# State-space layer of a hybrid encoder: the order of the setup's end, of the last group's gating and weight splits, and the place of the gate's store

## The chip, the cores and the metric
One Trainium2 chip, one core. The metric is device time in microseconds (us) of one execution of the whole two-layer network. Runs of one kernel shown below lie within 0.2% of each other.

## The reference, cut to what matters
Layer 0 is attention, layer 1 the bidirectional state-space mixer (Mamba-2 form), both with modulation before and a layer norm after:

```python
mod = cond @ ada_w[i] + ada_b[i]
shift, scale, gate = jnp.split(mod, 3, axis=-1)
h = x * (1.0 + scale[:, None, :]) + shift[:, None, :]
y = mixer(h)
x = _layer_norm(DEEPNORM_ALPHA * x + gate[:, None, :] * y, ln_g[i], ln_b[i])
```

```python
proj = h @ w_in                       # (1024, 2048 z + 3072 xBC + 64 dt)
xbc = silu(conv5(xbc) + conv_b)       # centred depthwise conv
dt_f, dt_b = softplus(...)            # one decay per head and direction
y = ssd(x, dt_f, B, C) + flip(ssd(flip(x), flip(dt_b), ...)) + d_skip * x
y = _rms_norm(y * jax.nn.silu(z), norm_w)
return y @ w_out                      # (2048 -> 1024)
```
The scan runs in 8 chunks of 128 tokens: inside a chunk `cb * lmat` (a masked product of C and B times a decay matrix) and across chunks a state that is decayed and added. There are 4 groups of 8 heads with a head size of 64 and a state of 128. All is float32.

## The kernel before
A float32 product is done as three matmuls of rounded parts: each operand is split in a rounded part (`w_hi`, `h_hi`, by ScalarE) and a remainder (`w_lo`, `h_lo`, by GpSimd or VectorE). Each engine has its own program, in the order in which the code issues it, with counting semaphores between them; all DMAs are issued by SP in one order.

**End of the attention layer.** For each of 8 tiles of 128 tokens VectorE, ScalarE and GpSimd normalise the projected tile; SP loads the residual rows (`load_x`, L393, buffer qT of two), stores the finished tile (L422), and behind tile 3 stores the next layer's gate (L427 to L430): 1024 values that lie on 128 partitions x 8 go to one row of 1024 in HBM, with `allow_slow_non_contiguous`. Only the very end of the kernel reads that row (L1783).

**Setup of the state-space layer.** TensorE projects 12 units (6 tiles of weights by 2 halves of the tokens) for group 0. ScalarE writes the centre tap (`first_centre`), VectorE adds the other taps (`first_unit`). Then, `for i in range(8)`, TensorE transposes one chunk (`unstage`), ScalarE copies it (`unstaged`), GpSimd scales it (`decayed_inputs`), TensorE makes the chunk's state (`state`) and VectorE adds it to the decayed one before (`update`, L2472). `update(0, k)` for k from 2 overwrites a buffer of hb that SP must have stored first (`keep_hb`, L1650). SP issues the weights w6 and w7 (`load_w`; w7 waits until w6 is split by GpSimd), and behind them the five stores of hb. `products` makes the products of C and B for four chunks each, `mask_products` (VectorE) masks them, `shift`, `lesser` and `exponentials` make the decay matrices, GpSimd's `weights_back` and VectorE's `weights` multiply the two. `skip` (ScalarE) puts d_skip * x into y.

**Groups.** A loop over groups 0 to 2 and the last one written out. Each goes through 8 chunks c; TensorE interleaves quarters of the next projections with each chunk's products (`quarter`, `outputs`). SP loads for chunk c+2 the decay rows (1 MB, L1637), the exponentials (L1643) and the stored hb (L1739). In the last group the quarters are those of z (8 units, `silu_half` on ScalarE and `silu_z` on VectorE).

**Behind the last group.** y is gated (8 instructions of VectorE, L2687), stored transposed (`send`), and loaded again tile by tile (`load_y(n)`, n counting pairs (m, c) of token tile and half of the channels in ORDER: (0,0), (1,0), (2,0), (0,1), (1,1), (2,1), (3,0), (3,1), ...). `split_y`/`y_rest` split it, `split_o`/`o_rest` split the 16 row blocks of w_out, `square` and GpSimd's `sum_squares` make the norm. TensorE's `out_products(m, k)` is 6 matmuls of 128 x 512. It first runs tiles 0, 1 and 2 together over k (blocks 0 to 15), as weights arrive, and then m = 3 to 7 one by one. A tile's accumulator `acc(m)` has two banks, of three pairs in turn; `normalise(m)` (L2724) reads it and frees it.

## Time and profile before

| | us |
|---|---|
| runs shown | 2201.43, 2200.47, 2197.43 (median 2200.47) |
| profiled execution, its time | 2194.47 |
| its span | 2192.7 |
| TensorE busy | 2094.6 (96%) |
| VectorE busy | 1035.6 (47%) |
| ScalarE busy | 948.0 (43%) |
| GpSimd busy | 832.9 (38%) |
| mean granted clock of TensorE | 0.993 |

Times inside the span are counted from its start. Engines in the rows: PE = TensorE, DVE = VectorE, ACT = ScalarE, POOL = GpSimd, SPq = SP's DMA queue. L12 is line 12 of the kernel before. "Busy" of TensorE comes from modelled ends of pipelined matmuls. The attention layer ends at about 1307 in the span, the setup at 1413, the groups follow at 1413.7, 1574 and 1735, the last one is at 1896 to 1985, and the output projection runs to the end.

### The profile page before, as it was taken

To read this page: it belongs to the slowest core of one execution; us is meant where nothing else is said; L and a number is where in the kernel's file an instruction comes from. 1 tells how busy PE (TensorE), PEld (TensorE's weight loads), DVE (VectorE), ACT (ScalarE), POOL (GpSimd) and SP (SyncE) were. 2 spreads that over 40 slices of the span, in tenths; PEclk is the share of its full clock that TensorE was granted. 3 is DMA by queue.
4 is the path that set the end of the run, shared out by engine and by line. 5 is a ranking of instruction groups with operands and counts; after the bars stand their busy time and mean duration, and the time that the engine had idled before them with its cause. 6 is when DMAs were issued, how large, how long until landed. Compare 5 with 4: busy or idle time off the path is not lost.

```text
span 2192.7 us, 33044 instructions
## 1 busy us (share of the span) xinstructions
PE 2094.6 (96%) x11587; PEld 1681.3 (77%) x11587; DVE 1035.6 (47%) x2305; ACT 948.0 (43%) x2354; POOL 832.9 (38%) x444
## 2 busy tenths in 40 slices
PE   4999999999999999999998989899999999998997
PEld 3888888887878888888776767688778778777776
DVE  6323223332233232232323566688487587477553
ACT  3243433434333343343435235565475565575220
POOL 0211141411412314114134163466376465484463
PEclk9999999999999999999999999999999999999998
DMA  7312221221222112112122341455254255356331
GB/s 306 129 39 66 58 71 38 69 67 30 67 67 69 67 39 59 67 51 85 38 62 66 119 116 53 139 166 163 94 181 154 104 164 157 105 182 214 141 113 58
DMA packets 98949, 221.26 MB, mean 101 GB/s; under 512 B 18850, under 2 KB 45090, under 8 KB 97316
## 3 DMA queue, kind: packets, MB, share of 16 engines
q1 hardware_dynamic: 98852, 219.98, 31.8%
q8 instruction: 59, 0.97, 0.2%
q14 instruction: 38, 0.31, 0.0%
HBM read 195.75 MB, written 24.19 MB: 100 GB/s over the span
## 4 chain that ended last, share of the span: by engine, by line
PE 68%; POOL 9%; issue 9%; DVE 7%; DMA 4%; ACT 3%; SPq 0%; POOLq 0%; DVEq 0%; ACTq 0%
PE pp L504 40%; PE pp_s L1926 7%; PE tp L536 4%; PE sp_ L526 3%; PE yo_p L2120 2%; PE op L609 2%; POOL rw L1824 2%; POOL trunk L1834 2%; POOL xw L1817 2%; PE pp_s L2120 1%; PE op L598 1%; DVE stage_s L2528 1%; POOL xd L1810 1%; PE tp L545 1%; DMA a_slot<-in_ada_w 1%
## 5 line engine op out<-in xcount | busy, mean ns | idle before, releaser
L437 POOL TENSOR_TENSOR w_lo<-w_raw,w_hi 128x1024 fp32r<-128x1024 f32 x80 | 190.6, 2382 | 847.6 <-ACT w_hi L765 847.6
L504 PE MATMUL pp<-h_hi,w_hi 128*128 128x512 f32 x1264 | 501.1, 396 | 0.1
L504 PE MATMUL pp<-h_hi,w_lo 128*128 128x512 f32 x1264 | 492.8, 390 | 0.0
L504 PE MATMUL pp<-h_lo,w_hi 128*128 128x512 f32 x1264 | 492.2, 389 | 0.0
L1035 DVE COPY probT<-tp 128x512 f32<-128x512 f32 x160 | 103.1, 685 | 544.9 <-PE tp L536 544.9
L1926 PE MATMUL pp_s<-h_hi,w_hi_s 128*128 128x512 f32 x624 | 270.7, 434 | 9.4 <-DVE stage_s L2528 7.4
L504 PEld LDWEIGHTS pp<-h_hi,w_hi 128*128 128x128 f32 x1264 | 237.4, 188 | 51.2 <-issue 4.8
L504 PEld LDWEIGHTS pp<-h_hi,w_lo 128*128 128x128 f32 x1264 | 237.2, 188 | 50.7
L504 PEld LDWEIGHTS pp<-h_lo,w_hi 128*128 128x128 f32 x1264 | 237.7, 188 | 46.7
L826 ACT ACTIVATE prob<-prob,mz 128x256 f32<-128x256 f32 (+2 forms) x384 | 169.9, 444 | 191.6 <-DVE mz L1015 191.6
L1926 PE MATMUL pp_s<-h_hi,w_lo_s 128*128 128x512 f32 x624 | 245.4, 393 | 0.0
L1926 PE MATMUL pp_s<-h_lo,w_hi_s 128*128 128x512 f32 x624 | 245.0, 393 | 0.0
L1926 PEld LDWEIGHTS pp_s<-h_hi,w_hi_s 128*128 128x128 f32 x624 | 117.9, 189 | 52.4 <-issue 26.7
L1575 POOL TENSOR_TENSOR w_lo_s<-w_raw_s,w_hi_s 128x1024 fp32r<-128x1024 f32 x40 | 104.8, 2619 | 122.8 <-ACT w_hi_s L1585 122.2
L2528 DVE SCALAR_TENSOR_TENSOR stage_s<-pp_s,gconv,stage_s 128x512 f32<-128x512 f32 (+2 forms) x184 | 137.8, 749 | 11.8 <-ACT stage_s L2168 6.1
L1926 PEld LDWEIGHTS pp_s<-h_lo,w_hi_s 128*128 128x128 f32 x624 | 118.1, 189 | 32.0 <-issue 10.6
L1926 PEld LDWEIGHTS pp_s<-h_hi,w_lo_s 128*128 128x128 f32 x624 | 117.8, 189 | 26.3
L1015 DVE CUSTOM_DVE_ANT_0 prob<-sp_,bias,slope 128x256 f32<-128x256 f32 (+2 forms) x384 | 134.3, 407 | 5.9 <-PE sp_ L526 3.6
L1035 DVE COPY v<-tp 128x512 f32<-128x512 f32 x48 | 30.9, 685 | 197.7 <-PE tp L545 197.7
L1817 POOL TENSOR_TENSOR xw<-trunk,fac 128x512 f32<-128x512 f32 x53 | 72.6, 1371 | 100.5 <-PE st_p L1941 88.7
L770 ACT ACTIVATE vT<-pp 128x512 f32<-128x512 f32 (+2 forms) x56 | 44.6, 812 | 137.2 <-PE pp L504 134.8
L2230 ACT ACTIVATE rw<-rw,fac 128x128 f32<-128x128 f32 x256 | 78.3, 389 | 41.4 <-DVE rw L2463 41.4
(453 smaller groups left out, 3547.7 us busy)
## 6 DMA issues: line engine op xcount, KB each, us to landing
w_raw<-in_a_w SPq DMA_DIRECT2D x80, 512.0 KB, 3.4
rw<-cum_rows SPq DMA_DIRECT2D x32, 1024.0 KB, 5.6
w_raw_s<-in_b_w SPq DMA_DIRECT2D x40, 512.0 KB, 3.5
ew<-exp_rows SPq DMA_DIRECT2D x64, 256.0 KB, 4.8
num_wide<-in_ada_w SPq DMA_DIRECT2D x16, 768.0 KB, 6.6
num_wide<-merge_rows SPq DMA_DIRECT2D x16, 768.0 KB, 7.8
yT_b<-trunk SPq DMA_DIRECT2D x32, 256.0 KB, 2.3
stage_s<-yT_b SPq DMA_DIRECT2D x16, 512.0 KB, 5.5
```

The costliest lines, as they stand in the source:

```text
L437: nc.gpsimd.tensor_tensor(w_lo[:, slot].rearrange("p k c -> p (k c)"), w_raw[:, slot].rearrange("p k c -> p (k c)"), w_hi[:, slot].rearran ...
L504: last = nc.tensor.matmul(pp[:, par, :], w[:, slot, k, :], keep[h][:, k, half * HALF:(half + 1) * HALF], start=(k == 0 and n == 0), stop=( ...
L536: last = nc.tensor.transpose(tp[:, par, c * P:(c + 1) * P], prob[:, u % 2, c * P:(c + 1) * P], ident[:])
L826: last = nc.scalar.activation(prob[:, u % 2, c:c + w], prob[:, u % 2, c:c + w], ACT.Exp, scale=-1.0, bias=mz[:, m:m + 1], accum_out=mz[:, ...
L1015: last = nc.vector.tensor_tensor_reduce(out=prob[:, u % 2, c:c + w], in0=sp_[:, u % 2, c:c + w], in1=bias[:, c0:c0 + w], scale=slope[:, h: ...
L1035: nc.vector.tensor_copy(dst, src).then_inc(t_free, 2 if ev[0] == "e" or ev[0] == "s" and last_pair else 1)
L1575: nc.gpsimd.tensor_tensor(flat(w_lo[:, slot]), flat(w_raw[:]), flat(w_hi[:, slot]).bitcast(F32), ALU.subtract).then_inc(S["lo_done"], 1)
L1817: nc.gpsimd.tensor_tensor(per_head(xw_of(n, k)), per_head(x[:, c, :]), bcast(f_in[:, c, d, :], HD), ALU.mult).then_inc(S["xw_ready"], 1)
L1926: last = nc.tensor.matmul(out, w[:, slot, k, :], of_h(h, k, half), start=(k == 0 and n == 0), stop=(k == KT - 1 and n == 2))
L2120: ins = nc.tensor.matmul(acc(m, half), y, w[:, half * HALF:(half + 1) * HALF], start=(k == 0 and i == 0), stop=(k == KO - 1 and i == 2))
L2230: last = nc.scalar.activation(rw[:, c % 2, 1, h, :], rw[:, c % 2, 1, h, :], ACT.Exp, bias=f_bias[:, c, h:h + 1])
L2528: ins = nc.vector.scalar_tensor_tensor(out, src[:, a - 2 + k - half * HALF:b - 2 + k - half * HALF], w[:, k:k + 1], out, ALU.mult, ALU.add)
```

## The change
Eight edits:
1. SP: the gate's store goes from behind tile 3 of the attention layer into the last group, behind the loads of c = 3.
2. Setup, ScalarE: `split_hi(6)` behind copy 2 instead of ahead of copy 0; `exponentials(0, 0)` and `inputs(0, 0)` ahead of the four skips. GpSimd: `split_lo(6)` behind `decayed_inputs(0, 2)`.
3. Setup, VectorE: updates 4 and 5 and `lesser` ahead of the first masked products, update 6 ahead of the second. TensorE: `state(0, 6)` between the two `products`.
4. Last group: y0 is loaded at c = 2, and y1, w_out blocks 0 and 1 at c = 5 and later; y0 is split ahead of chunk 7's exponentials, the others within c = 6 and 7. Buffers: y_raw(1) in rw, y_hi of n = 1 and 2 exchanged, acc of m = 0 and 2 exchanged.
5. The gating goes over the first half of the tokens for all four kt, then the second; only the first four sends are waited for before y3, the others before n = 9.
6. TensorE: the first six blocks in the order (k, m) = (0,0), (1,0), (0,1), (1,1), (0,2), (1,2), and blocks 13 to 15 tile by tile.
7. y4 and y5 are split together behind w_out block 9, and squared behind both.
8. For m from 3 on, y is loaded, split and squared one tile earlier (at m = 0 for the loads and m = 1 for the splits).

```diff
@@ attention, SP @@
                     if m == 1:
                         after["load"](sp, 1)
-                    if m == 3:
-
-                        sp.wait_ge(n_set, 2)
-                        sp.wait_ge(gate_out, 16)
-                        sp.dma_start(io["gate_row"][1].rearrange("(k p) -> p k", p=P), mods[:, 1, 2 * KT:3 * KT],
-                                     allow_slow_non_contiguous=True).then_inc(gate_out, 16)
@@ state space, names @@
-        y_hi = [w_hi[:, 0], w_hi[:, 1], y_hi_2[:, 0], y_hi_2[:, 1]]
+        def y_raw(n):
+
+            return rw[:, 0, 0] if n == 1 else stage[:, 4 + n % 2].rearrange("p (k c) -> p k c", k=KT)
+        y_hi = [w_hi[:, 0], y_hi_2[:, 0], w_hi[:, 1], y_hi_2[:, 1]]
...
-            return (pp[:, half, :], yo_p[:, half, :], (st_p, fill)[half][:])[m % 3]
+            return ((st_p, fill)[half][:], yo_p[:, half, :], pp[:, half, :])[m % 3]
@@ SP @@
+                def send_last(i):
+
+                    kt, hf_ = i % 4, i // 4
+                    wait(sp, "y_gated", 8 * LAST + (i + 1))
...
+                                 ).then_inc(half_out if hf_ == 0 else y_out[kt], 16)
...
                     elif n == 1:
-                        wait(sp, "yo_full", CH * LAST + CH)
+                        wait(sp, "yd_full", CH * LAST + CH - 1)
...
-                    if n in (0, 3):
+                    if n == 0:
                         for kt in range(4):
-                            sp.wait_ge(y_out[kt], 32 * (2 * c + 2))
+                            sp.wait_ge(y_out[kt], 64)
+                    if n == 3:
+
+                        sp.wait_ge(half_out, 64)
...
+                        if last and c == 2:
+                            load_y(0)
+                        if last and c == 3:
+
+                            sp.wait_ge(first["n_set"], 2)
+                            sp.wait_ge(first["gate_out"], 16)
+                            sp.dma_start(io["gate_row"][1].rearrange("(k p) -> p k", p=P),
+                                         keep["mods"][:, 1, 2 * KT:3 * KT],
+                                         allow_slow_non_contiguous=True).then_inc(first["gate_out"], 16)
                         if last and c == 5:
-                            load_y(0)
+                            load_o(0)
                         if last and c == 6:
-                            load_o(0)
+                            load_y(1)
...
                 load_o(1)
-                load_y(1)
                 load_o(2)
                 load_y(2)
                 load_o(3)
                 load_o(4)
-                for i in range(8):
-                    send(LAST, i)
-                    if i in (1, 3, 5):
-                        load_o(5 + i // 2)
+                for i in range(6):
+                    send_last(i)
+                load_o(5)
                 load_y(3)
-                load_y(4)
-                for k in range(8, KO):
+                for i in range(6, 8):
+                    send_last(i)
+                for k in range(6, KO):
                     load_o(k)
-                    if k == 10:
-                        load_y(5)
+                    if k in (6, 9):
+                        load_y(4 + k // 8)
@@ GpSimd @@
-                for f in range(XB - 1):
+                for f in range(4):
                     split_lo(pool, f + 2, f % 2)
-                    if f < 4:
-                        silu(f)
+                    silu(f)
                 pool.wait_ge(fac_in, 16)
                 for k in range(7):
                     wait(pool, "xu_free", k + 1)
                     decayed_inputs(0, k)
+                    if k == 2:
+                        split_lo(pool, 6, 0)
@@ TensorE @@
-                for b in range(2):
-                    products(0, b)
+                products(0, 0)
                 state(0, 6)
+                products(0, 1)
...
-                wait(pe, "v_done", CH * LAST + CH)
-                wait(pe, "z_done", 8)
-                for k, ms in [(0, (0, 1)), (1, (0, 1)), (0, (2,)), (1, (2,))] + [(k, (0, 1, 2)) for k in range(2, KO)]:
+                for k, ms in ([(k, (m,)) for m in range(3) for k in (0, 1)] + [(k, (0, 1, 2)) for k in range(2, KO - 3)]
+                              + [(k, (m,)) for m in range(3) for k in range(KO - 3, KO)]):
                     pe.wait_ge(o_lo_done, k + 1)
                     for m in ms:
+                        if (k, m) == (0, 1):
+                            wait(pe, "u_done", CH * LAST + CH)
+                        if (k, m) == (0, 2):
+                            wait(pe, "z_done", 8)
@@ ScalarE @@
-                split_hi(act, 6, 0)
...
                     unstaged(0, i)
+                    if i == 2:
+                        split_hi(act, 6, 0)
+                exponentials(0, 0)
+                inputs(0, 0)
                 for kt in range(4):
                     skip(0, kt)
-                exponentials(0, 0)
-                inputs(0, 0)
...
                                 shift(j, c + 1)
+                                if c == 6:
+                                    split_y(0)
                                 exponentials(j, c + 1)
                                 inputs(j, c + 1)
                             if c == 6:
-                                split_y(0)
+                                split_o(0)
+                                split_o(1)
+                                split_y(1)
@@ VectorE @@
                 update(0, 3)
-                mask_products(0, 0)
                 update(0, 4)
                 lesser(0, 0)
+                update(0, 5)
+                mask_products(0, 0)
+                update(0, 6)
                 mask_products(0, 1)
-                update(0, 5)
-                update(0, 6)
                 weights(0, 0)
...
                             silu_z(c - 1)
+                            if c == 6:
+                                y_rest(0)
+                            if c == CH - 1:
+                                o_rest(1)
                         assemble(j, c)
                         if c + 1 < CH:
                             weights(j, c + 1)
                         if last and c == 6:
-                            y_rest(0)
+                            o_rest(0)
+                        if last and c == CH - 1:
+                            y_rest(1)
...
                         for i in range(8):
-                            yv = y[:, i // 2, i % 2 * HALF:(i % 2 + 1) * HALF]
+                            kt, half = i % 4, i // 4
+                            yv = y[:, kt, half * HALF:(half + 1) * HALF]
...
-                            if i % 2:
-                                o_rest(2 + i // 2)
+                            if i == 3:
+                                y_rest(2)
+                            if i % 2 and i > 3:
+                                o_rest(i // 2)
+                        for k in range(4, 6):
+                            o_rest(k)
```

## Rows read from the trace of the kernel before
**Rows 1.** Stretch view: bounds, length, busy (instructions) by engine, clock, DMA share, GB/s.
```profile
1413.70:1574.00 160.30, 158.59 (x929) 127.94 (x928) 120.55 (x222) 92.51 (x260) 90.35 (x54) 0.99 0.47 143
...
1980.00:2030.00 50.00, 42.51 (x206) 34.56 (x205) 37.28 (x31) 25.49 (x27) 24.99 (x20) 0.97 0.68 218
```
**Rows 2.** Waits of TensorE, 1896 to 2193: who for whom, us, times, longest.
```profile
PE pp_s L2120 <- DVE h_lo L2714: 5.3, 1, 5.3
PE yo_p L2120 <- DVE w_lo_s L2719: 3.9, 2, 2.4
PE st_p L2120 <- DVE w_lo_s L2719: 2.2, 1, 2.2
PE pp_s L2120 <- DVE us L2736: 2.0, 1, 2.0
```
**Rows 3.** Timeline of SP's queue: start, duration, line, what it issues.
```profile
1280.36 0.38 SPq L429 DMA_DIRECT2D gate_row<-mods  x1
1280.78 1.04 SPq L393 DMA_DIRECT2D qT<-in_x  x1
```
**Rows 4.** DMA view of 1281 to 1293: packets by size.
```profile
DMA packets 1343, 1.13 MB, mean 94 GB/s; under 512 B 1070, under 2 KB 1070, under 8 KB 1342
```
**Rows 5.** Line L393, loads of residual rows: issue to landing.
```profile
DMA to landing us min/median/max: 4.1/5.3/13.1
```
**Rows 6.** Timelines of VectorE and TensorE, with the idle time before and its releaser.
```profile
1293.86 1.23 DVE L1251 SCALAR_TENSOR_TENSOR trunk<-qT,trunk 128x1024 f32<-128x1024 f32 x1 [6.88 <-DMA qT<-in_x]
...
1299.52 1.11 PE L1596 MATMUL pp_s<-ident,trunk 128*128 128x128 f32 x4 [7.33 <-ACT rw L1605]
...
1307.05 0.47 PE L1926 MATMUL pp_s<-h_hi,w_hi_s 128*128 128x512 f32 x1 [1.54 <-DVE h_lo L1617]
```
**Rows 7.** Stretch view of single us: length, TensorE busy, clock, DMA share, GB/s.
```profile
2067.00:2068.00 1.00, 1.00 (x4) 0.50 0.84 328
...
1299.00:1300.00 1.00, 0.48 (x3) 0.50 0.00 0
```
**Rows 8.** Timeline of SP's queue in the last group.
```profile
1948.18 0.59 SPq L1739 DMA_DIRECT2D hb<-hb_s  x1
1953.39 0.38 SPq L1637 DMA_DIRECT2D rw<-cum_rows  x1
```
**Rows 9.** Issues of 1953.3 to 1953.5: count, KB, us to landing.
```profile
rw<-cum_rows SPq DMA_DIRECT2D x1, 1024.0 KB, 5.3
```
**Rows 10.** Timelines of ScalarE and VectorE in the last group.
```profile
1958.88 2.44 ACT L2223 ACTIVATE rw<-rw,fac 128x128 f32<-128x128 f32 x8
...
1963.50 1.75 DVE L2463 TENSOR_TENSOR rw<-rw 128x1024 f32<-128x1024 f32 x1
```
**Rows 11.** Timelines of GpSimd, TensorE and VectorE at the setup's end.
```profile
1392.68 2.37 POOL L1575 TENSOR_TENSOR w_lo_s<-w_raw_s,w_hi_s 128x1024 fp32r<-128x1024 f32 x1 [11.50 <-ACT w_hi_s L1585]
...
1393.40 0.66 PE L1981 MATMUL fill<-ident,stage_s 128*128 128x128 f32 x4 [1.68 <-ACT bt L2157]
...
1412.98 1.68 PE L1941 MATMUL st_p<-xw,bt 128*128 128x512 f32 x2 [2.05 <-DVE hb L2486]
...
1402.90 1.62 DVE L2486 SCALAR_TENSOR_TENSOR hb<-hb,fac,st_p 128x64 f32<-128x64 f32 x8
...
1411.22 1.61 DVE L2486 SCALAR_TENSOR_TENSOR hb<-hb,fac,st_p 128x64 f32<-128x64 f32 x8
```
**Rows 12.** Issues of 1370 to 1440, stores of hb: count, KB, us to landing.
```profile
hb_s<-hb SPq DMA_DIRECT2D x5, 256.0 KB, 2.0
```
**Rows 13.** Timeline of TensorE, first block of k = 2 in the output projection.
```profile
2000.13 0.62 PE L2120 MATMUL pp_s<-h_hi,w_hi_s 128*128 128x512 f32 x2
```
**Rows 14.** Lines L2719 and L2687: duration in ns min/median/max, first and last start.
```profile
L2719 DVE TENSOR_TENSOR y_lo<-stage_s,y_hi x8: 1224/1662/2320, 1994.7 to 2147.2; 128x1024 fp32r<-128x1024 f32 x8
...
L2687 DVE SCALAR_TENSOR_TENSOR trunk<-stage_s,trunk x8: 677/816/1784, 1995.8 to 2007.3; 128x512 f32<-128x512 f32 x8
```

More of the change, by code:

```diff
@@ L1786, in _ @@
                         load_x(m + 2)
-                    if m >= 2 and 2 * m + 5 < 2 * MT:
-                        load_y(2 * m + 4)
-                        load_y(2 * m + 5)
+                    if 2 * m + 9 < 2 * MT:
+                        load_y(2 * m + 8)
+                        load_y(2 * m + 9)
                     sp.wait_ge(out_ready, m + 1)
@@ L1916, in _ @@
                     affine(m)
-                    if m >= 2 and 2 * m + 5 < 2 * MT:
-                        sum_squares(2 * m + 4)
-                        sum_squares(2 * m + 5)
+                    if m >= 1 and 2 * m + 7 < 2 * MT:
+                        sum_squares(2 * m + 6)
+                        sum_squares(2 * m + 7)
             @block.tensor
@@ L1929, in project_k @@
                         last.then_inc(S["pp_full"], 1)
+                    return last
                 def project(par, tile, slot, half, part):
@@ L1934, in project @@
                     for k in (2 * part, 2 * part + 1):
-                        project_k(pp[:, par, :], slot, half, k)
+                        ins = project_k(pp[:, par, :], slot, half, k)
+                    return ins
                 def state(n, k):
@@ L2069, in quarter @@
                                 wait(pe, "pp_free", free + (u - 1))
-                        project(u % 2, 10 * j + (XB + u // 2), u // 2 % 2, u % 2, q % 4)
+                        ins = project(u % 2, 10 * j + (XB + u // 2), u // 2 % 2, u % 2, q % 4)
+                        if last and q == 28:
+                            ins.then_inc(first_read, 1)
                     for c in range(CH):
@@ L2436, in _ @@
                 split_o(6)
-                split_o(7)
                 split_y(3)
                 square(3)
-                for k in range(8, KO):
+                for k in range(7, KO):
                     split_o(k)
-                    if k in (10, 11):
-                        split_y(k - 6)
-                        square(k - 6)
+                    if k == 9:
+                        for n in (4, 5):
+                            split_y(n)
+                        for n in (4, 5):
+                            square(n)
                 for n in range(6, 8):
@@ L2452, in _ @@
                     nc.scalar.activation(ln_sd[:, 1:2], ln_sd[:, 0:1], ACT.Sqrt).then_inc(root_done, 1)
-                    if m >= 2 and 2 * m + 5 < 2 * MT:
-                        for n in range(2 * m + 4, 2 * m + 6):
+                    if m >= 1 and 2 * m + 7 < 2 * MT:
+                        for n in range(2 * m + 6, 2 * m + 8):
                             split_y(n)
@@ L2757, in _ @@
                 o_rest(6)
-                o_rest(7)
                 y_rest(3)
-                for k in range(8, KO):
+                for k in range(7, KO):
                     o_rest(k)
-                    if k in (10, 11):
-                        y_rest(k - 6)
+                    if k == 9:
+                        y_rest(4)
+                        y_rest(5)
                 for n in range(6, 8):
@@ L2768, in _ @@
                     normalise(mt)
-                    if mt >= 2 and 2 * mt + 5 < 2 * MT:
-                        for n in range(2 * mt + 4, 2 * mt + 6):
+                    if mt >= 1 and 2 * mt + 7 < 2 * MT:
+                        for n in range(2 * mt + 6, 2 * mt + 8):
                             y_rest(n)
```

46 lines of the change are left out of this document (27 added, 19 removed).

## The prediction
> **What bounds the kernel now.** I read the stretch view first: in the loop over the groups TensorE is busy 158.6 of 160.3 us in the first of them [rows 1], so nothing off TensorE is worth much there. The holes lie at four places, and the change touches all four. After the last group: 42.5 of 50 us busy in 1980 to 2030 [rows 1]. The list of waits names its holes: 5.3 us for the first remainder of the output weights (h_lo, L2714), 3.9 and 2.2 us for remainders of y (L2719), 2.0 us for an accumulator that the normalisation had not read (L2736) [rows 2]; for yo_p the 3.9 are 1.55 at 2027.7 and 2.37 at 2090.6. Then, by the timelines, three places where I followed a wait back to its cause: the end of the attention layer, the end of the state-space setup, and the sixth chunk of the last group. The profiled execution took 2194.47 us (span 2192.7); the median of the runs shown is 2200.47. I take savings from the profile and apply them to the median.
>
> **1. The gate's store leaves the attention layer.** SP issues it at 1280.36, and 0.4 us behind it the load of residual rows qT for tile 6 [rows 3]. The store writes single elements: in 1281 to 1293 there are 1070 packets under 512 B at a mean of 94 GB/s [rows 4]. The load behind it lands after 13.1 us, where such loads have a median of 5.3 and a least of 4.1 [rows 5]. VectorE waits 6.88 us for it (1293.86) [rows 6], ScalarE's modulation of the transposed columns stands behind that tile's root, and so TensorE waits 7.33 us at 1299.52 [rows 6] and then runs at half clock (0.50, the 1.2 GHz level) [rows 7]: its matmuls come every 0.43 us instead of 0.227. Without the store: load at 1280.3 + 5.3 = 1285.6, VectorE's tile 6 reaches L1251 at 1287.0, 6.9 us earlier. TensorE's transpose comes at 1292.5, 7.0 earlier, hardly idle, so at full clock; its last work before the roundings (1305.5) takes 4 instead of 6 us. The eight roundings, the eight remainders and the next layer's first projection (1307.05) [rows 6] come 7.0 + 1.9 = **8.9 us** earlier. What is next late: nothing; the last tile's row load goes out at 1288.5 and has until 1303. Bounds: 6.9 (the clock falls anyway) to 9.
>
> **2. The gate's store enters the last group.** It now stands behind the load of hb at chunk 3, issued 1948.18 [rows 8], so goes out at about 1948.8. It has the same packets. In the old place it blocked until about 1292.3, 11.9 us after its issue (bytes per us rise again only then); here that is 1960.7. Behind it on the queue is the 1 MB load of rows for chunk 6, issued 1953.39 [rows 8], which lands 5.3 us later when nothing is ahead [rows 9] and about 3 us of that is transfer: so it lands at 1963.5 to 1965.5 instead of 1958.7. ScalarE's eight shifts (2.44 us) started at 1958.88 and would end at 1966 to 1968; VectorE takes their result at 1963.50 [rows 10], so 2.2 us of slack go first. VectorE's next step behind it, silu_z(4), releases TensorE's quarter 24 with no slack (1965.91), and the masked weights of chunk 6 follow the same shift. Cost 2.5 to 4.5; I take **3.5**. Bounds: 0 (rows come just in time) and 8.9 (all that it cost before).
> The Trainium skill (DMA: Bandwidth & Descriptors, Rules for kernel authors) says that a non-contiguous last dimension becomes one descriptor for each element. By this rule the store is as dear in the new place as in the old, and only slack can make it cheaper; with no slack the sum below would be 5.4 us worse. The packets agree with the rule.
>
> **3. End of the setup.** (a) The split of w6 waited 3.5 us for its load on ScalarE ahead of the first copies; TensorE waited 1.68 us at 1393.40 for the copy [rows 11]. Behind three copies it is free on ScalarE: it takes 1.05 us of a wait of 1.26 before copy 3. TensorE's chain of state 0 starts 2.2 us earlier, since xw no longer stands behind the split of w6 on GpSimd (1392.68, 2.37 us) [rows 11]. (b) But this split's lower half now ends at 1400.3 instead of 1395.05, and SP's load of w7 waits for it; behind that load on SP is the first store of hb, which lands 2.0 us after issue [rows 12]. So the store goes from 1398.0 to 1400.7 and lands at 1402.7, if the 0.5 MB load ahead of it doesn't hold it (then 1404.7). Update 2 overwrites that buffer; it began at 1402.90 [rows 11]. So it gains 0.15 or loses 1.8, and the head start of (a) is gone there. (c) What is then won is the order on VectorE: update 4 began at 1411.22, behind a wait for the products [rows 11]; now it follows update 3 at 1407.1 and ends at 1408.7. State 6 moves between the two products (1409.75), products end at 1411.7, and the group's first projection starts there instead of at 1413.67: 2.0 us. (d) The exponentials go ahead of four skips (4.1 us), 1409.9 to 1412.3 instead of 1414.0 to 1416.4; the masks end at 1415.3, GpSimd's weights start then instead of at 1416.59. ScalarE's whole queue still ends at 1418.3, so its work in chunk 0 isn't earlier. (e) TensorE ran its first 2.9 us of the group at the same half clock; shorter holes may spare 1.5. Bounds: -2 and +4 (2.0 + 1.5 + slack); I take **+2**, nearest to what the order alone gives, the block behind state 6 at 1412.98 [rows 11].
>
> **4. The output projection.** The split of y0 falls into ScalarE's wait ahead of chunk 7's exponentials (3.1 us), its remainder on VectorE into a wait of 2.67. So at 1982.85 VectorE starts on the first weight's remainder (1.85) and TensorE can start as the last chunk ends, 1985.04, where it waited 5.3 us [rows 2]. But the projection then outruns VectorE. From 1982.85: o0 1.85, silu 0.6, o1 1.7, chunk 7 1.25, y1 2.25, silu 0.6, four gatings 3.6, y2 1.2 to 2.3, two gatings 1.6, o2 1.3 to 2.3 (the remainders of y and the gatings [rows 14], the rest by the timeline of 1982 to 2009), so o2 ends at 1998.8 to 2000.9. TensorE's six short blocks (1.36 each) are done as their operands come, with holes of 0.6, 2 and 3 us, and k=2 starts at about 1999.7 instead of 2000.13 [rows 13]: 0.4 us of the 5.3 come back, the rest is turned into later holes. After that the gain is real. Only the first four sends (half the tokens) are needed by y3; they are gated by 1994.5 instead of 2008, so load_y(3) goes out at about 2000 and not 2014.09, and the holes of 1.55 and 2.24 at k=8 close: 3.8 us. Splits 4 and 5 wait for part_done (2021.5, 2022.8), in time for 2025.5 and 2026.9; o10, now behind two squares and a sum on GpSimd (3.4 to 5.3 us), comes at 2031.9 for 2032.4: no hole, or one of 1.4. Finishing tile 0 six blocks early lets its normalisation begin at 2048.8 with tiles 1 and 2 (8.2 us) for cover: the accumulator is free at 2054.2, needed at 2057: 2.0 us [rows 2], and the half clock behind it (2065.3 to 2068.7, 0.50 [rows 7], 1.6 us) goes too. y8 and y9 are loaded and split one tile earlier: the last 2.37 at 2090.60 [rows 2]. Sum 0.4 + 3.8 + 2.0 + 1.6 + 2.4 = **10.2**. Bounds: 6 (half clock stays, o10 late, VectorE's long durations) and 13 (short durations).
> VectorE's remainder of y takes 1.22 us alone and 2.3 beside GpSimd [rows 14], and I used both. The Trainium skill (GPSIMD Engine Reference, Specifications) says that GpSimd shares its SBUF interfaces with VectorE and collides with VectorE instructions that have two SBUF inputs; by it all of y1, y2 and the gatings are at the long duration, o2 ends at 2000.9, and the sum is 0.8 smaller.
>
> **Sum.** 8.9 - 3.5 + 2 + 10.2 = 17.6: 2194.5 becomes 2177, and the median 2200.5 becomes 2183.
>
> **Rivals.** (A) The store costs in the last group what it cost before (8.9) and SP's queue turns the setup into a loss of 2: 8.9 - 8.9 - 2 + 10.2 = 8.2, so 2192. For: the same packets, the row load right behind, and the store of hb behind a later load on SP. Against: the 4.6 us between store and load, and ScalarE's slack. (B) The store is hidden, the clock stays up and VectorE runs at short durations: 9 - 0 + 4 + 13 = 26, so 2174.5. (C) The holes are only moved: VectorE, 37.3 of 50 us busy there, bounds the projection, and the residual load is slow by its neighbours and not by the store: 2200. Against: two loads ahead of it took 4 to 5 us beside the same stores. (D) Slower: the elements' store meets the 1 MB broadcast loads of the last group and drags them out over several chunks. Place: rows of chunks 6 and 7, ScalarE's shifts. Each us beyond 4.6 us of lateness goes to TensorE. To undo the other terms (21) rows must be 26 us late, so the store would have to block some 35 us, three times as long as seen; then 2205. Against: nothing in the old place suggests it.
>
> **Chances.** Forecast 0.68 (own range 2178 to 2188), A 0.14, B 0.12, C 0.03, D 0.03. A difference under 0.2% (4.4 us) can't be told from none. Faster: forecast, A and B, 0.94; same 0.03, slower 0.03. Range 2174 to 2191.
>
> **What would show it.** 1: the row load of tile 6 lands in under 6 us and TensorE has no wait over 1 us at L1596. 2: the shift of chunk 6 waits for rw, 4 to 6 us. 3: update 2 begins at a store of hb; update 4 directly behind update 3. 4: TensorE's first projection block follows the last chunk at once; holes of 0.6 to 3 us up to k=2, none at k=8, L2736 and y8. The prediction is wrong if the load stays at 13 us, if a hole remains at k=8, or if chunk 6 stalls over 6 us.

## The result, and the profile after

The changed kernel took 2187.09 us (median of 5 runs, 2182.03 to 2190.51) against 2198.38 for the kernel before beside it: ratio 0.9942, 95% interval 0.9926 to 0.9958. So it is faster by 11 (by the medians) to 13 us (by the ratio; interval 9 to 16). 2183 was predicted, in a range of 2174 to 2191, with 0.94 on faster. The profiled executions differ by less, spans of 2186.3 and 2192.7 us. The ledger below is made from these two, so it adds up to 6.4 us. The profiled execution of the kernel before (2194.47 us) is faster than all five of its timed runs (2197.43 to 2201.43), that of the changed kernel (2188.09) is 1 us above its median; in which stage the other 5 to 6 us lie no profile shows.

The stretch view of the changed kernel, to set against [rows 1] (bounds, length, busy by engine, clock, DMA share, GB/s):

```profile
1413.70:1574.00 160.30, 156.01 (x919) 126.10 (x918) 114.95 (x207) 89.92 (x246) 87.93 (x53) 0.99 0.46 142
1980.00:2030.00 50.00, 46.41 (x222) 37.96 (x219) 36.03 (x31) 24.81 (x33) 27.12 (x18) 0.93 0.66 221
```

In the same 50 us TensorE is busy 3.9 us more, though at a granted clock of 0.93 and not 0.97. In the window of the first group it is busy 2.6 us less, though the code of the loop is the same. The group had begun 4.6 us earlier, so the two windows don't hold quite the same work. The waits of TensorE from 1896 on, against [rows 2] (who for whom, us, times, longest):

```profile
PE pp_s L1952 <- DVE stage_s L2691: 5.4, 3, 5.1
PE pp_s L2151 <- DVE y_lo L2771: 3.6, 1, 3.6
```

All four waits of [rows 2] are gone, h_lo, both of w_lo_s and the accumulator. Two new ones stand there: 5.1 us in the last group, at a projection quarter that waits for silu_z (L2691), and 3.6 us for the remainder of y2.

**Attention layer.** The load of residual rows behind the store's old place ([rows 3, 5, 6] before), in the timelines of SP, VectorE and TensorE (start, us, ..., idle before and its releaser), and the remainders h_lo by tile (min/median/max ns, first and last start):

```profile
1280.53 0.43 SPq L393 DMA_DIRECT2D qT<-in_x  x1
...
1287.32 2.08 DVE L1245 SCALAR_TENSOR_TENSOR trunk<-qT,trunk 128x1024 f32<-128x1024 f32 x1
...
1293.83 0.66 PE L1594 MATMUL pp_s<-ident,trunk 128*128 128x128 f32 x4 [1.42 <-ACT rw L1603]
...
1300.13 0.47 PE L1952 MATMUL pp_s<-h_hi,w_hi_s 128*128 128x512 f32 x1 [2.44 <-DVE h_lo L1615]
```

```profile
L1615 DVE TENSOR_TENSOR h_lo<-rw,h_hi x16: 678/682/1589, 1298.4 to 1324.0; 128x512 fp32r<-128x512 f32 x16
```

The load lands after 3.8 us and VectorE doesn't wait for it at all, the hole of 7.33 us is one of 1.42, and no half clock follows. The next layer's first projection starts 6.9 us earlier, at 1300.13 and not 1307.05.

The median of 5.3 us in [rows 5] is that of the six loads from 1248.9 on. The two before them (1222.65) took 12.4 and 13.1 us with no such store ahead, but behind some 3 MB of other loads and with the engines moving 197 GB/s or more; so a landing after 13 us alone doesn't prove the store, and e1 below has to.

**Setup's end** ([rows 11, 12] before), SP's and VectorE's timelines:

```profile
1393.29 0.34 SPq L1561 DMA_DIRECT2D w_raw_s<-in_b_w  x1
1393.68 0.43 SPq L1650 DMA_DIRECT2D hb_s<-hb  x1
```

```profile
1397.92 1.24 DVE L2527 SCALAR_TENSOR_TENSOR hb<-hb,fac,st_p 128x64 f32<-128x64 f32 x6 [4.80 <-DMA hb_s<-hb]
```

The first store of hb stands behind the load of w7. The buffer's contents were ready at 1388.3; the store goes out at 1393.68 and lands 4.2 us later. Update 2 waits 4.80 us for it and TensorE 3.69 for the update. Behind that hole TensorE runs at half clock for some 7 us, up to just ahead of the group's first projection (1409.05):

```profile
1401.00:1407.00 6.00, 5.20 (x19) 3.69 (x18) 5.57 (x24) 2.20 (x7) 1.63 (x2) 0.50 0.24 92
```

**Last group.** ScalarE's shift of chunk 6 and TensorE's quarter behind it ([rows 8 to 10] before), then the clock of two stretches:

```profile
1946.38 0.38 SPq L1763 DMA_DIRECT2D gate_row<-mods  x1
1950.98 0.38 SPq L1635 DMA_DIRECT2D rw<-cum_rows  x1
...
1964.11 2.44 ACT L2257 ACTIVATE rw<-rw,fac 128x128 f32<-128x128 f32 x8 [7.54 <-DMA rw<-cum_rows]
...
1968.46 0.79 PE L1952 MATMUL pp_s<-h_hi,w_hi_s 128*128 128x512 f32 x1 [5.12 <-DVE stage_s L2691]
```

```profile
1968.00:1974.00 6.00, 5.54 (x11) 3.72 (x12) 3.38 (x4) 6.00 (x22) 3.64 (x3) 0.50 0.54 171
1999.00:2005.00 6.00, 5.73 (x14) 4.51 (x15) 6.00 (x6) 2.06 (x2) 4.68 (x4) 0.50 0.60 172
```

The row load takes 13.1 us (5.3 before [rows 9]). Behind the hole of 5.12 TensorE runs at 0.50 (the 1.2 GHz level) until 1974, and again behind the 3.59 us for y2 at 1999.27. The last chunk ends at 1989.92. It was 2.4 us ahead of the kernel before when the rows were issued, and is 4.9 behind now: the store costs 7.3 us in this execution. Some of it comes back: the operands of the output projection have had more time, and from the issue of these rows to the end of the span the change takes 235.3 us where e3 below, with the store elsewhere, takes 229.2. So 6.1 us are the net price.

**Output projection.** From the last chunk's end to the end of the span the kernel before needs 207.7 us and this one 196.4: 11.3 gained. From the first block of k=8 on TensorE has no wait, and the 11.1 us won there are all of it but 0.2.

### The profile page after: what moved, and what is told of

The parts are those of the page before. It is cut to its first block, busy times and chain, and to the rows that moved or that the text cites. A ratio compares the mean times of both kernels' runs of the same rounds, so it can differ in the third digit from the quotient of the medians.

```text
span 2186.3 us, 33046 instructions
## 1 busy us (share of the span) xinstructions
PE 2097.0 (96%) x11587; PEld 1683.6 (77%) x11587; DVE 1028.9 (47%) x2305; ACT 947.0 (43%) x2354; POOL 836.5 (38%) x444
## 4 chain that ended last, share of the span: by engine, by line
PE 78%; issue 7%; DVE 6%; POOL 5%; DMA 2%; ACT 2%; SPq 0%; POOLq 0%; DVEq 0%; ACTq 0%
PE pp L498 40%; PE pp_s L1952 12%; PE tp L530 4%; PE sp_ L520 3%; PE yo_p L2151 3%; PE op L603 2%; PE pp_s L2151 2%; PE st_p L2151 1%; PE fill L2151 1%; POOL xw L1842 1%; PE op L592 1%; POOL rw L1849 1%; PE st_p L1969 1%; PE yd_p L1997 1%; PE tp L539 1%
## 5 line engine op out<-in xcount | busy, mean ns | idle before, releaser
L2569 DVE SCALAR_TENSOR_TENSOR stage_s<-pp_s,gconv,stage_s 128x512 f32<-128x512 f32 (+2 forms) x184 | 137.9, 749 | 12.6 <-ACT stage_s L2202 7.1
L1952 PEld LDWEIGHTS pp_s<-h_lo,w_hi_s 128*128 128x128 f32 x624 | 118.6, 190 | 31.9 <-issue 10.1
```

The lines of the kernel that those rows point to most:

```text
L1952: last = nc.tensor.matmul(out, w[:, slot, k, :], of_h(h, k, half), start=(k == 0 and n == 0), stop=(k == KT - 1 and n == 2))
L2569: ins = nc.vector.scalar_tensor_tensor(out, src[:, a - 2 + k - half * HALF:b - 2 + k - half * HALF], w[:, k:k + 1], out, ALU.mult, ALU.add)
```

## The experiments

Each kernel was timed 5, 6 or 12 times beside the kernel before. Ratios are to that kernel on the same chip (2196.70 us for e1 to e4, 2202.78 for e5 to e8, 2198.22 for e9 to e12), with 95% intervals. Four facts of each profile stand in one table: how far ahead of the profile of the kernel before (positive: earlier) four events come. They are SP's issue of the cum_rows store in the setup (before: 1367.75), of the last load of rows that the first group issues (1516.64; the group itself runs on to 1574), of the rows for chunk 6 in the last group (1953.39), and the end of the span (2192.7).

```
kernel                       ratio (interval)         setup  group 1  last gr.  end
change                       0.9942 (0.9926-0.9958)    6.9     2.4      2.4     6.4
e1  before, store in setup   0.9969 (0.9955-0.9983)    6.6     6.9      6.0     3.5
e2  before, store last group 0.9997 (0.9982-1.0012)    7.6     4.3      5.3    -2.9
e3  change, store in setup   0.9916 (0.9892-0.9940)    5.2     1.2      4.5    14.6
e4  e3, w7 behind stores     0.9902 (0.9884-0.9921)    5.4     7.9      8.5    18.5
e5  e3, old setup order      0.9894 (0.9874-0.9913)    5.7     6.3      4.0    14.2
e6  e4, convolution first    0.9918 (0.9901-0.9936)    6.3     4.1     -2.1     7.3
e7  change, ScalarE's queue  0.9921 (0.9904-0.9938)    6.9     4.6      3.1    10.3
e8  change, store behind o0  0.9922 (0.9905-0.9939)    7.1     5.2     -0.1     8.5
e9  e4, gatings later        0.9895 (0.9882-0.9909)    5.2     5.0      7.6    18.9
e10 e5, gatings later        0.9908 (0.9894-0.9921)    5.4     7.1      5.7    17.0
e11 e10, w7 behind           0.9915 (0.9902-0.9927)    6.5     7.5      7.3    19.1
e12 e3, gatings later        0.9923 (0.9911-0.9935)    6.6     3.1      6.9    18.7
```

**The store.** Edit of e1 (and of e3, from the changed kernel): out of the attention layer (or the last group), and, with the arguments of the store cut short here,

```diff
                 for n in range(2, 6):
                     load_w(sp, n)
+                    if n == 2:
+                        sp.wait_ge(first["n_set"], 2)
+                        sp.wait_ge(first["gate_out"], 16)
+                        sp.dma_start(io["gate_row"][1]..., keep["mods"][:, 1, 2 * KT:3 * KT], ...)
```

> The kernel before, with one edit: the gate's store leaves the attention layer and goes out behind the load of w2 in the state-space setup, where SP issues nothing for 25 us and the DMA engines stand at 0 GB/s. Theory: the end of the attention layer comes 7 us earlier, as it did in the changed kernel (first projection of the next layer at 1300.1 instead of 1307.1), and the store costs nothing in the new place. Of the 7 us the loop over the groups gives back part: in the changed kernel the lead went from 6.6 us (1451) to 2.4 (1841). So 2192 to 2195 if the loop takes 3 to 4 us whatever comes in, and 2191.4 (7 us) if the loop's loss was chance. Rival (the residual load is slow by its neighbours, not by the store): 2198, and the load behind it still takes 13 us.

Measured 2190.78 against 2196.70, 6.8 us by the ratio (3.7 to 9.9). The residual load behind the store's old place lands after 4.0 us instead of 13.1, so it was slow by the store. The setup is 6.6 us ahead and the loop keeps 6.0 of it, so the loop as such does not take a lead back (2190.8 for the 2191.4 expected of that case).

e2 is the kernel before with the store at the change's place:

> The kernel before, with the gate's store moved from the attention layer to the last group (behind the load of hb at chunk 3), as the change has it, and nothing else. Theory: 7 us are won at the attention layer's end; in the last group the 1 MB load of rows behind the store takes 13 us instead of 6, TensorE stalls 5 us at a projection quarter and then runs about 5.7 us at half clock, 7.3 us in all. Against the kernel with the store in the setup this is 7 us more: 2197 to 2202, so no faster than the kernel before. Rival (my forecast: 3.5 us in the last group): 3.5 us more than with the store in the setup.

2196.26, no gain. The rest of the change is not in it, and yet the rows of chunk 6 land after 12.5 us, ScalarE waits 6.88 us for them and TensorE 4.46 at the quarter behind:

```profile
1960.54 2.44 ACT L2224 ACTIVATE rw<-rw,fac 128x128 f32<-128x128 f32 x8 [6.88 <-DMA rw<-cum_rows]
```

```profile
1964.89 0.79 PE L1927 MATMUL pp_s<-h_hi,w_hi_s 128*128 128x512 f32 x1 [4.46 <-DVE stage_s L2651]
```

Against e1 the last group's place costs 0.0028 of the time or 6 us: the store's move, taken by itself, gave back what it won.

> The whole change, but the gate's store in the setup behind the load of w2. Theory: no wait for rw in the last group, no half clock behind it: 7.3 us less than the changed kernel's 2187.1, so 2179 to 2181. Rival 1: the stall gave VectorE and GpSimd time to catch up, and the output projection has more holes without it: 3 to 5 us of the 7.3 come back, 2183 to 2185. Rival 2: the row load is slow there without the store: 2187.

2177.47, 18.4 us under the kernel before (13 to 24), against some 12.7 for the change: again 6 us, and the case of 2187 falls; that of 2183 to 2185 is out by the median, not by the whole interval. In e3's profile the rows of chunk 6 land after 5.2 us, ScalarE starts their shift with no wait (1954.41), and TensorE goes from the last chunk into the output projection in 0.2 us.

e7 issues the store from ScalarE's queue, e8 leaves it on SP's but behind the load of the first output weight:

> The changed kernel, but the gate's store in the last group is issued by ScalarE (on its own DMA queue, chunk 4) and not by SP. Theory A (the loads behind it on SP's queue stand in line behind its 1024 packets): the row load of chunk 6 lands in 6 us, and the time is that of the kernel with the store in the setup, 2177 to 2180. Theory B (the store keeps the DMA engines themselves busy, whatever queue it is on): the row load issued within its 12 us is as late as before, 2184 to 2188.

> The changed kernel, but the gate's store stands behind the load of the first output weight (chunk 5 of the last group), after which SP issues nothing for 9 us. Theory: what the store costs is decided by how soon a load follows that is needed at once; here the next ones (y1 and o1) go out 9 us later and would be late by 2 to 4 us, hidden in VectorE's backlog: 2178 to 2182. Rival (any place in the last group costs 6 us or more): 2184 to 2188.

e7: 2183.66 against 2202.78. The median can't tell the theories apart: 0.9921 overlaps e3's interval and the change's. The trace can. Timeline of ScalarE and SP, then the stretch view of the same kernel:

```profile
1942.60 0.39 ACTq L2367 DMA_DIRECT2D gate_row<-mods  x1
...
1950.26 0.39 SPq L1635 DMA_DIRECT2D rw<-cum_rows  x1
...
1961.58 1.57 ACT L2250 ACTIVATE rw<-rw,fac 128x128 f32<-128x128 f32 x5 [5.71 <-DMA rw<-cum_rows]
```

```profile
1945.00:1948.00 3.00, 3.00 (x22) 2.75 (x21) 2.37 (x4) 3.00 (x9) 3.00 (x3) 1.00 0.79 8
1948.00:1951.00 3.00, 3.00 (x39) 2.58 (x39) 3.00 (x9) 0.79 (x3) 3.00 (x2) 1.00 0.65 10
```

The row load on SP's own queue, with the store on another, takes 11.3 us to land, and the core's DMA engines, busy for 0.65 to 0.79 of the time, move 8 to 10 GB/s. So it isn't SP's queue alone that is blocked: theory B, with a smaller price; the load went out 7.7 us behind the store and not 4.6. From the issue of these rows to the end e7 takes 232.1 us, the change 235.3 and e3 229.2, so 2.9 us for the store, by one trace each. The Trainium skill (DMA: Bandwidth & Descriptors, Issuing engines are not separate DMA queues) has the rule, that DMAs of all issuing engines run on the same 16 engines and interleave; the trace agrees.

e8: 2184.15, which is the rival's time (2184 to 2188) and not the theory's; its ratio can't be told from e7's. Its loop came out badly (no lead left at the last group), which nothing in its edit touches. By the same stretch the store itself costs 1.6 us (230.8 against 229.2), so the trace speaks for the theory and the median doesn't: where in the last group the store costs least stays open. The loads of y1 and o1 went out only 5 us behind it, since chunk 6 did not stall; o1 came late (ScalarE waits 3.07 us for it), and TensorE's second block waits 2.27 us for its remainder.

**The setup's end.** e4 changes the order on SP alone:

```diff
                 load_w(sp, 6)
-                load_w(sp, 7)
                 for k in range(5):
                     keep_hb(0, k)
+                load_w(sp, 7)
```

> The kernel with the whole change and the gate's store in the setup, and SP's load of w7 behind the five stores of hb at the setup's end instead of ahead of them. Theory: the first store waits on SP behind the load, which waits for the lower half of w6; update 1 was ready at 1388.3, the store went out at 1393.7 and landed at 1397.9, where update 2 waited 4.8 us for it. Without this, update 2 begins at about 1393.2, TensorE's wait of 3.7 us and the half clock behind it go, and the group starts 3.5 to 5 us earlier: 2175 to 2177 if the loop keeps the lead, 2179 to 2181 (as the one before) if the loop gives it back, which would show that what comes in early is lost in the loop.

Update 2 starts at once:

```profile
1389.86 0.34 SPq L1650 DMA_DIRECT2D hb_s<-hb  x1
...
1394.76 1.43 DVE L2526 SCALAR_TENSOR_TENSOR hb<-hb,fac,st_p 128x64 f32<-128x64 f32 x7
```

e3 has it at 1399.92 behind a wait of 5.08, and is 1.2 us ahead of the kernel before at the last load of rows in the first group; e4 is 7.9 ahead. TensorE's clock stays at 1.00 there, and the group's first projection starts at 1405.08, 8.6 us before that of the kernel before: of the 5.4 us that e4 was ahead when the setup's end began, nothing is lost, and 3.2 are added. The time, 2176.14, is 1.3 us below e3's 2177.47, within the intervals, so the sum stayed open here. e5 puts the setup's end back as it was (the split of w6, the order of updates, products, skips and exponentials):

> The kernel with the whole change and the gate's store in the setup, but with the setup's end put back as it was in the kernel before (split of w6, order of updates, products, skips and exponentials). Two readings: against the same kernel with the new setup's end (2177.5) it gives what the setup's edits are worth, and against the kernel before with only the store in the setup (2190.8) what the edits of the output projection are worth. Theory 1 (the loop takes back what is early): the new order starts the group 2 us earlier in the profile but its fourth chunk waits for VectorE's convolution whatever comes in, and in the traces the kernels with the new order have lost 3.5 to 5 us by 1478 that the kernels with the old one keep: so this kernel is faster than 2177.5 by 1 to 3 us. Theory 2 (those losses are chance): it is slower by 1 to 2 us. Output projection by either: 2190.8 minus 10 to 12.

2178.89 against 2202.78 on its chip: 0.9894, better than e3's 0.9916 by 4.8 us, though from another chip and with overlapping intervals. In its trace TensorE has no wait over 0.5 us in the first group. The second reading was of the output projection: against e1 the edits of the last group and behind it are worth 11.9 us by the medians, 16.5 by the ratios (two chips) and 10.7 in the profiles, where 10 to 12 were expected.

The last four runs had all of this on one chip: the setup's order (new or old) crossed with the place of w7 (ahead of the stores or behind them), and one new step in all:

```diff
-                            if i == 3:
+                            if i == 1:
                                 y_rest(2)
-                            if i % 2 and i > 3:
-                                o_rest(i // 2)
+                            if i in (3, 5):
+                                o_rest((i + 1) // 2)
```

> One of four kernels with the gate's store in the setup and the change's output projection; they differ in the order of the setup's end (the change's or the old one) and in the place of SP's load of w7 (behind or ahead of the five stores of hb). This one: the change's order, w7 behind. All four also have one new step: VectorE's remainder of y2 comes behind two gatings and not four, and the remainders of the third and fourth weight ahead of the last four gatings. In the kernels so far TensorE waited 3.7 us for the remainder of y2 and ran 3 to 4 us at half clock behind it. Theory for that step: the hole falls to 1.6 us or less, the clock stays up, 3 to 5 us less than without it, so about 2172. Rival: the hole moves to the third weight, which comes behind the gatings: no gain, 2176. Theory for the setup: only with w7 behind the stores is the new order worth its effort: this kernel beats the same with w7 ahead by 3 to 4 us.

> The old order at the setup's end, w7 ahead of the stores of hb, gate's store in the setup, output projection with the remainder of y2 behind two gatings. Theory: in the traces the old order loses 0 to 1 us between the setup and the end of the first group, the new one with w7 ahead 2 to 4.5 us; so this one is 1 to 3 us faster than the new order with w7 ahead, and within 2 us of the new order with w7 behind. Rival (the setup's edits are worth the 2 us of my forecast): 2 us slower than the new order with w7 ahead.

> As the one before, but w7 behind the stores of hb. Theory: in the old order the stores waited for nothing on SP that mattered (update 2 had no wait for a store), so moving w7 changes nothing: within 1 us of the old order with w7 ahead. Rival (the place of w7 helps by itself, whatever the order): 2 to 4 us faster.

> The change's order with w7 ahead of the stores, as the change has it; gate's store in the setup; remainder of y2 behind two gatings. Theory: the slowest of the four by 1 to 3 us, about 2175, since update 2 waits 4.8 us for a store that stands behind the load of w7. Rival (the losses seen in the first group are chance): the four are within 1 us of each other.

Medians: e9 2174.95, e10 2177.43, e11 2179.05, e12 2179.93, the kernel before 2198.22. With the new order, w7 behind the stores is worth 5.0 us (the intervals just part; the pair of e3 and e4 had 1.3); with the old order it is worth nothing that can be measured (1.6 us the other way). The change's combination is the slowest of the four, 2.5 us behind the old order, and e9, the new order with w7 behind, is 2.5 us ahead of the old order as it was (e10): both differences are inside the intervals. The ends of the profiles don't rank the four this way (19.1 to 17.0 us ahead, e10 last). The stretch that the setup's end feeds does: between the cum_rows store and the last load of rows in the first group the five kernels with the change's combination (the change, e3, e7, e8, e12) lose 4.5, 4.0, 2.2, 1.9 and 3.5 us; those with the old order (e1, e2, e5, e10, e11) gain 0.3, 0.6, 1.7 and 1.0 and lose 3.4 once (e2); e4 gains 2.5, e9 loses 0.1.

The new step for y2: TensorE's hole falls from 3.7 to 2.5 us (in e9 up to 1987.79), since the two gatings ahead of it still take 2.83 us beside GpSimd, where four had taken 4.29, and the remainder 1.47; the clock stayed up in e11 and e12 but not in e9 and e10. In e11 and e12 a hole of 0.9 us for the third weight's remainder follows, as the rival had it. From the rows of chunk 6 to the end the step is worth 1.1 to 1.8 us (229.2, 229.3 and 229.1 without, 227.5 to 228.0 with), too little for the medians: the 3 to 5 us expected did not come. e9 has the lowest median here, 2174.95 (0.9895), and lies clear of the changed kernel; e5's ratio (0.9894, another chip) is as good.

**The loop.** In the first group of the change, of e3 and of e4 TensorE has a hole at the same place, the fourth to fifth chunk, where a quarter waits for VectorE's convolution, and half clock for a few us behind it (the change's rows):

```profile
1465.00 0.49 PE L1952 MATMUL pp_s<-h_hi,w_hi_s 128*128 128x512 f32 x1 [2.75 <-DVE stage_s L2569]
```

```profile
1464.00:1470.00 6.00, 5.00 (x15) 3.82 (x15) 5.72 (x7) 6.00 (x20) 5.47 (x3) 0.72 0.31 69
```

In the kernel before and in e1 this hole is 1.2 us in the first group and the clock stays up (1.20 us up to 1468.19, and 1.21 up to 1461.67). VectorE is the engine behind there (9.9 of 10 us busy in e4 from 1450 to 1460). But the hole is not the new order's alone: in the second and third groups it is 2.5 and 2.8 us in the kernel before, 2.8 and 2.8 in e1, and 1.6 and 2.8 in e4. An early start alone doesn't make it larger either: e1's first group starts at 1406.97, the change's at 1409.05, and e1 has the smaller hole. What does is open. e6 tried to take the hole away by moving the minimum behind that convolution:

> The fastest kernel so far (2176.1: store in the setup, w7 behind the stores of hb) with one step of VectorE's order changed in the groups that are not the last: at the fourth chunk the convolution comes ahead of the minimum of the masks (1.9 us) and not behind it. Theory: TensorE's hole of 2.7 us there waits for that convolution, and the half clock behind it costs another 1.5 to 2 us; the hole falls to 0.8 to 1.2 us, at which the clock stayed up in the kernel before's first group, so up to 3.5 us in each of three groups, 8 us in all if nothing else is late. Rival: ScalarE's exponentials, which wait for the minimum, come 3 us later, the centre of the next unit and the split behind them too, and the hole is only moved: no gain, or a loss of 1 us in each group.

2184.03, 0.9918 against e4's 0.9902, 3.5 us slower: the rival, though the intervals overlap (two chips). The traces are plainer. TensorE's waits for the convolution in the three groups are 14.8 us in e6 and 7.1 in e4. The hole comes a few us later as one of 3.8 us in each of the three groups (in the first up to 1473.55).

## Why the prediction was right, and which steps failed

The direction and the range held, and 2187.09 lies in the forecast's own range (2178 to 2188). But of the forecast's 17.6 us the profiles show 6.4 and the medians 11 to 13, and three of the four terms missed the same way: in the profiles the first came out 2.0 us worse, the second 3.8, the third and the first group behind it 6.5, and only the fourth 1.1 better. That the number still fell into the narrow range is in part luck: the kernel before ran 2 us faster beside the change than the median that the prediction started from (2198.38, not 2200.47), and the timed runs show 5 to 6 us more gain than the profiles, for which there is no account. The likeliest case came true in its first and fourth terms and not in the other two. Rival A (8.2 us: the store as dear as before, the setup a loss of 2) had the setup about right and is nearer for the store by the 7.3 of the trace (its net price, 6, lies midway), and the gain of 11 to 13 us is nearer to its 8.2 than to 17.6.

1. **Store out of the attention layer, 8.9 forecast, 6.9 in the change's profile, 5.2 to 7.6 (mean 6.3) by the first column of the table over the 13 kernels without it.** The mechanism was right in each step: load quick, no 7.33, no half clock (its 2 us came); the hole left at L1594, 1.42 us, is over the 1 us that was named as a sign. Two sizes were missed, both where GpSimd is busy once nothing waits. The modulation came 5.7 us earlier and not 7.0, since VectorE's sum with the residual started 0.3 us later than reckoned and took 2.08 us where it had taken 1.23 alone. And the first remainder of h takes 1.59 us instead of 0.68 beside GpSimd's last affine step (1297.07 to 1299.43), on the path. The Trainium skill's rule that the prediction used for y2 (GPSIMD Engine Reference, Specifications: GpSimd shares its SBUF interfaces with VectorE, and a VectorE instruction with two SBUF inputs collides) is the one that should have been applied here; the trace agrees with it (2.08 and 1.59 us beside GpSimd, 1.23 and 0.68 alone).

2. **Store into the last group, 3.5 forecast, 7.3 in the change's profile up to the last chunk, 6 by the medians (e2 against e1, the change against e3).** This is the term of the store that failed most. The store's effect lasts 12.6 us from its issue (11.9 forecast), and the rows came within 13.1 us of theirs (10.1 to 12.1 forecast). Of the 7.6 us by which chunk 6's shift was late, 2.2 were slack, and TensorE came 5.0 late: 1.5 more than the forecast. ScalarE waited 7.54 us for the rows, where 4 to 6 were named as the sign and a stall over 6 as a sign of being wrong; TensorE's own stall, 5.12, is under that line. What the prediction left out altogether is the half clock behind the stall, 2.3 to 2.8 us, though it had counted the same thing as a saving elsewhere. Rival A's price (8.9) was nearer to 7.3 than the forecast's.

3. **Setup's end, +2 forecast; -2.3 in the change's profile at the group's first projection (4.6 us ahead, where 6.9 came in); by the times -2.5 (e12 against e10) to -4.8 (e3 against e5), inside the intervals of each pair.** Step (b) named the mechanism, the store of hb behind the load of w7, "gains 0.15 or loses 1.8". Everything ahead of it was 6.92 us earlier, update 2 only 4.98: it came 1.94 late. But then (c) took the order's gain as though update 2's wait stood beside it and not in its chain; and (e) counted on the clock as a saving, where TensorE's hole of 3.69 us brought 6 us of half clock of its own (1401 to 1407). The order itself is worth what was forecast and more: up to the group's first projection e4 gains 3.2 us, and e9, which has w7 behind as well, gains 3.2 too, where e12 loses 1.7. The group's start was also taken for the end of the matter. The head start that did come (the first quarter 4.6 us ahead, the first rows 5.9) was down to 1.6 at the rows loaded at 1477.08 (1478.70 before), behind the hole of 2.75 us where TensorE waits for VectorE. The rows of the prediction had that bound only as 1.7 us of holes in the first group; in the second and third the kernel before waits 2.5 and 2.8 us at this place.

4. **Output projection, 10.2 forecast, 11.3 in the change's profile and 10.1 in e3's.** The difference between the two is what the stall of chunk 6 gave back. The steps hold one by one: k=2 starts 0.5 us earlier relative to the last chunk's end (0.4 forecast), the holes at k=8, at the accumulator and at y8 are gone (11.1 us from the first block of k=8 to the end; 9.8 forecast). Of the holes ahead of k=2 there was one of 3.6 us with half clock behind it, not three. e1's own tail is 2.5 us longer than that of the kernel before with the same code (its hole at y8 is 4.0 us and not 2.4), so against e1 the edits are worth 12.6 in the profiles.

So: 6.9, less 4.5 in the setup's end and the first group, nothing net in the other two (3.5 lost by 1677.73 and won back by 1841.40, times of the kernel before), less 7.3 and plus 11.3, 6.4 us. Rivals B, C and D are dead: the shift of chunk 6 waits 7.54 us, e1 frees the residual load, e3 shows the holes of the output projection closed and not moved, and in the change the store's effect ends with chunk 6. Open is what the loop does: kernels with the same setup leave it with leads between -0.1 and 6.9 us, and the runs of one changed kernel spread over 6 to 13 us. That the clock behind a hole of 1.4 to 2.8 us, which falls in some groups and not in others, makes this spread fits the traces but was not tested.

## What to carry to other kernels

Move a store that slows the DMA engines to where nothing is loaded while its effect lasts (here 12 us from its issue), not to where the queue merely looks short, and count what TensorE's clock costs behind each stall that a change brings in, as readily as behind each that it takes away. Reordering a chain of compute steps brings in the stores and loads that guard its buffers: their order on the issuing queue must be changed with it (here one line, worth 1.3 us in one pair of kernels and 5.0 in the other). An earlier start of a loop is no gain yet: e9 was 8.4 us ahead at the start of the first group and 5.0 ahead 100 us on. And compare a forecast with its parts: a number inside the range can hide terms that all missed the same way.

## What the hardware showed that was not expected

The store of 1024 single elements is over quickly as packets and yet slow for all that comes after. In the changed kernel's DMA view, the microsecond from 1949 on:

```profile
DMA packets 1060, 0.09 MB, mean 90 GB/s; under 512 B 1018, under 2 KB 1018, under 8 KB 1060
```

The four microseconds behind it have no packet at all, and the next five have 3 to 12 each, 12 to 49 GB/s, while a load of 1 MB issued at 1950.98 waits; 225 GB/s are back at 1959. In e7 it is 8 us (from 1945 to 1953 at 6 to 14 GB/s), and in the kernel before 8 as well (from 1284 to 1292 at 12 to 74 GB/s). What the engines do in that time no view shows, and whether the same 4 KB stored in one piece would be free of it was not tried. In the setup (e3, packets at 1318) no load follows for 20 us, and neither e1 nor e3 shows a wait for it.
